# End of the last block in halves and three column groups, accumulators added earlier, norms by square root and reciprocal, gates by tanh

## The reference, cut to what matters

```python
mix = token_mixer(x, ...)          # ends in  sigmoid(ga) * (o @ w_branch_a) + sigmoid(gb) * (yc @ w_branch_b), then @ w_out
x = layer_norm(ALPHA * x + mix, ln1_g, ln1_b)                       # "first norm"
x = layer_norm(ALPHA * x + peer(x, ...), ln2_g, ln2_b)              # "second norm"
x = x + sigmoid(x @ ple_w_gate) * (p @ ple_w_proj)                  # "final gate"

def layer_norm(x, g, b):           # (x - mean) * rsqrt(var + 1e-5) * g + b
def peer(x, w_q, sub_keys, u, v):  # per token: 8 heads x 16 experts found by top-k search over product keys
    h = gelu(sum_d u[e, d] * x[d])             # for each of the 128 experts e of the token
    return sum_e softmax_weight[e] * h[e] * v[e, :]
```

## Time and profile before

| | |
|---|---|
| median of 3 runs | 1919.62 us (1918.05 to 1920.31) |
| the profiled execution, own time | 1921.58 us |
| its span | 1919.5 us |
| busy: PE, DVE, ACT, POOL | 1620.7, 1293.0, 814.6, 487.8 us |
| gathers (queue q0) | 536.90 MB of 655.38 MB moved |
| mean granted clock of PE | 0.956 of full speed |

### The profile page before, as it was taken

The page is one execution under the profiler, slowest core; times in us unless marked ns, Lnnn a source line. Parts: engine busy times, 40 slices in busy tenths (PEclk is TensorE's granted clock), DMA queues, the critical chain, the costliest instruction groups (busy, mean ns, idle before and its releaser), DMA issues.

```text
span 1919.5 us, 17005 instructions
## 1 busy us (share of the span) xinstructions
PE 1620.7 (84%) x5048; PEld 898.7 (47%) x5048; DVE 1293.0 (67%) x2758; ACT 814.6 (42%) x1954; POOL 487.8 (25%) x530
## 2 busy tenths in 40 slices
PE   8999989779999899688978767778787778878787
PEld 6888867675555557344434322233222223222223
DVE  4453575169987679777777777776666677666643
ACT  6566574132147312534434434443444444344432
POOL 0000000022222122232333333333333333333330
PEclk9999999889999999899989988999999999999998
DMA  5112256789999989899999999999999999999992
GB/s 204 52 63 87 88 219 263 274 353 416 393 386 401 370 306 379 359 419 384 414 371 418 404 414 411 382 416 372 422 413 422 421 373 420 384 422 422 421 421 97
DMA packets 93925, 655.38 MB, mean 341 GB/s; under 512 B 10256, under 2 KB 13840, under 8 KB 15632
## 3 DMA queue, kind: packets, MB, share of 16 engines
q0 software_dynamic: 73728, 536.90, 68.6%
q1 hardware_dynamic: 20112, 117.48, 15.8%
HBM read 652.24 MB, written 2.10 MB: 341 GB/s over the span
## 4 chain that ended last, share of the span: by engine, by line
PE 41%; DMA 31%; ACT 11%; DVE 11%; issue 4%; POOL 1%; SPq 0%; ACTq 0%; DVEq 0%; POOLq 0%
DMA uv<-in_pk_uv,idx 29%; PE psum L1624 11%; PE psum L1530 11%; PE psum L1386 4%; DVE uv L1257 4%; PE psum L1549 4%; PE psum L1592 2%; PE psum L1563 2%; PE psum L1501 2%; PE psum L1482 2%; DVE oT L1270 1%; ACT diag L807 1%; DMA raw<-in_w_branch_a 1%; ACT L795 1%; ACT coef L799 1%
## 5 line engine op out<-in xcount | busy, mean ns | idle before, releaser
L1624 PE MATMUL psum<-uv,diag 128*128 128x512 f32 x1424 | 732.1, 645 | 229.5 <-ACT diag L807 225.9
L1257 DVE CUSTOM_DVE_ANT_0 uv<-uv,psum 128x1024 f32<-128x1024 f32 x512 | 622.4, 1216 | 318.8 <-DMA uv<-in_pk_uv,idx 312.6
L573 POOL DMA_INDIRECT uv<-in_pk_uv,idx x512 | 484.3, 946 | 1387.8 <-DVE oT L1270 494.0
L1624 PEld LDWEIGHTS psum<-uv,diag 128*128 128x128 f32 x1424 | 263.1, 200 | 668.4 <-ACT diag L807 442.3
L795 ACT ACTIVATE gelu<-dots 128x1 f32<-128x1 f32 x512 | 103.5, 202 | 787.8 <-DVE dots L1257 785.9
L1530 PE MATMUL psum<-xT,raw 128*128 128x384 f32 x640 | 206.6, 486 | 0.0
L1270 DVE SCALAR_TENSOR_TENSOR oT<-uv,coef,oT 128x1024 f32<-128x1024 f32 x152 | 194.3, 1279 | 15.7 <-ACT coef L799 15.7
L1530 PEld LDWEIGHTS psum<-xT,raw 128*128 128x128 f32 x640 | 121.6, 190 | 84.5
L799 ACT ACTIVATE coef<-gelu,weight 128x1 f32<-128x1 f32 x512 | 150.9, 295 | 16.9 <-ACT gelu L795 0.2
L807 ACT ACTIVATE diag<-ident,coef 128x128 f32<-128x128 f32 x356 | 143.0, 402 | 11.7
L1386 PE MATMUL psum<-xTh,w_hi 128*128 128x512 f32 x256 | 105.4, 412 | 9.3 <-DVE xTl L984 9.3
(11 more groups left out here) (199 smaller groups left out, 1668.3 us busy)
## 6 DMA issues: line engine op xcount, KB each, us to landing
raw<-in_w_in SPq DMA_DIRECT2D x56, 1024.0 KB, 6.8
raw<-in_pk_w_q SPq DMA_DIRECT2D x16, 1024.0 KB, 8.8
raw<-in_w_branch_a SPq DMA_DIRECT2D x8, 1024.0 KB, 7.3
raw<-in_w_branch_b SPq DMA_DIRECT2D x8, 1024.0 KB, 6.8
raw<-in_w_out SPq DMA_DIRECT2D x8, 1024.0 KB, 10.1
uv<-in_pk_uv,idx POOLq DMA_INDIRECT x512, 9.8
w_gate<-in_ple_w_gate SPq DMA_DIRECT2D x1, 4096.0 KB, 13.8
x_raw<-in_x_t SPq DMA_DIRECT2D x4, 512.0 KB, 7.3
```

The source lines that it names most:

```text
L573: pool.indirect_dma_start(uv[:, r % UV, :], None, pk_uv, bass.IndirectOffsetOnAxis(idx[:, i % 2, j:j + 1], 0)).then_inc(row_in[r % UV], 16)
L1257: V.tensor_tensor_reduce(u, u, x_cur[:], 1.0, 0.0, ALU.mult, ALU.add, dots[:, r % 32:r % 32 + 1]).then_inc(dot_done, 1)
L1624: last = T.matmul(B[i][:], diag[:, n % DR, :], uv[:, r % UV, D + i * 512:D + (i + 1) * 512], start=(r in FIRST), stop=(k == BLOCK_ROWS - 1 ...
```

## The change

- **Gates.** The sigmoids of `unit_out` and of the final gate become tanh(x/2); since sigmoid(x) = (1 + tanh(x/2))/2, the multiplications by a gate become one instruction (gate + 1) times the other factor. The doubled `mix` of blocks 1 to 3 is met by `2.0 * ALPHA` and an epsilon of 4e-5 in their first norm (`twice`); the final gate's half is in the last addition. The sigmoids of the mixer ahead of the loop stay.
- **Norms.** `rstd_of` becomes `root_of` (one Sqrt on ACT) and a reciprocal on DVE, which stands in DVE's order just ahead of the shift.
- **Accumulators.** `add_acc` of blocks 1, 2 and 3 moves from row 126 of the block to rows 118, 44 and 44.
- **Halves.** PE signals `v_half` after the first 512 columns of a block's last row; `fin_sum` adds each half when it is there. In the last block the shift, the transposes and the start of the gate matmuls go by halves too.
- **Last gate in three groups** of 512, 256 and 256 columns: matmuls, tanh, multiplication, addition and store of one group after another, with the last group in bank 2.

```diff
-        ACC_ROW = [BLOCK_ROWS * (b + 1) - 2 for b in range(TB)]
+        ACC_ROW = [BLOCK_ROWS * b + t for b, t in enumerate((BLOCK_ROWS - 2, 118, 44, 44))]
+        LAST_PARTS = [(0, 512), (512, 768), (768, 1024)]
+        LAST_BANK = (6, 7, 2)
...
-            store(3)
-            sp.wait_ge(stored, 16 * TB)
+            for i, (d0, d1) in enumerate(LAST_PARTS):
+                sp.wait_ge(x3_done, TB + i)
+                sp.dma_start(ov[:, TB - 1, d0:d1], x2[:, d0:d1]).then_inc(stored, 16)
+            sp.wait_ge(stored, 16 * (TB + len(LAST_PARTS) - 1))
...
-                    nc.scalar.activation(t[:, c, P:], src, ACT.Sigmoid).then_inc(t_act, 1)
+                    nc.scalar.activation(t[:, c, P:], src, ACT.Tanh, scale=0.5).then_inc(t_act, 1)
...
-                nc.scalar.activation(rstd[:, 0:1], mean_var[:, 1:2], ACT.Ln, bias=eps_ln[:, 0:1]).then_inc(rst, 1)
-                act.wait_ge(rst, 2 * n + 1)
-                nc.scalar.activation(rstd[:, 1:2], rstd[:, 0:1], ACT.Exp, scale=-0.5).then_inc(rst, 1)
+                nc.scalar.activation(rstd[:, 0:1], mean_var[:, 1:2], ACT.Sqrt,
+                                     bias=eps_ln[:, twice:twice + 1]).then_inc(root, 1)
...
-                nc.scalar.activation(gate[:, i * 512:(i + 1) * 512], B[6 + i][:], ACT.Sigmoid).then_inc(g_sig, 1)
+                nc.scalar.activation(gate[:, i * 512:(i + 1) * 512], B[6 + i][:], ACT.Tanh, scale=0.5).then_inc(g_sig, 1)
...
-            for i in range(2):
-                gate_sigmoid(TB - 1, i)
+            for i, (d0, d1) in enumerate(LAST_PARTS):
+                act.wait_ge(g_mm, 2 * (TB - 1) + i + 1)
+                nc.scalar.activation(gate[:, d0:d1], B[LAST_BANK[i]][:, 0:d1 - d0], ACT.Tanh, scale=0.5).then_inc(g_sig, 1)
...
-                V.tensor_tensor(g, g, B[bank(r)][:, 0:n], ALU.mult).then_inc(t_dve, 1)
+                V.scalar_tensor_tensor(out=g, in0=g, scalar=1.0, in1=B[bank(r)][:, 0:n],
+                                       op0=ALU.add, op1=ALU.mult).then_inc(t_dve, 1)
...
+            def norm_rstd(n, root, rec):
+                dve.wait_ge(root, n + 1)
+                V.reciprocal(rstd[:, 1:2], rstd[:, 0:1]).then_inc(rec, 1)
...
-                dve.wait_ge(v_used, v_count(BLOCK_ROWS * (b + 1) - 1))
...
                 for i in range(2):
                     d = slice(i * 512, (i + 1) * 512)
+                    if i == 0:
+                        dve.wait_ge(v_half, b + 1)
+                    else:
+                        dve.wait_ge(v_used, v_count(BLOCK_ROWS * (b + 1) - 1))
                     V.scalar_tensor_tensor(out=x2[:, d], in0=x_of(b)[:, d], scalar=ALPHA, in1=B[i][:],
                                            op0=ALU.mult, op1=ALU.add).then_inc(acc_out, 1)
...
-                norm_shift(b, x2[:], ln2[1], x2_step, x2_rstd, x2_done)
+                norm_rstd(b, x2_root, x2_rec)
+                if b < TB - 1:
+                    norm_shift(b, x2[:], ln2[1], x2_step, x2_rec, x2_done)
+                else:
+                    for i in range(2):
+                        d = slice(i * 512, (i + 1) * 512)
+                        norm_shift(b, x2[:, d], ln2[1][:, d], x2_step, x2_rec, x2_done)
...
-                V.tensor_tensor(gate[:, d], gate[:, d], B[pb][:], ALU.mult).then_inc(fin_step, 1)
+                V.scalar_tensor_tensor(out=gate[:, d], in0=gate[:, d], scalar=1.0, in1=B[pb][:],
+                                       op0=ALU.add, op1=ALU.mult).then_inc(fin_step, 1)
...
-                V.tensor_tensor(x2[:], x2[:], gate[:], ALU.add).then_inc(x3_done, 1)
+                V.scalar_tensor_tensor(out=x2[:], in0=gate[:], scalar=0.5, in1=x2[:],
+                                       op0=ALU.mult, op1=ALU.add).then_inc(x3_done, 1)
...
-            for i in range(2):
-                fin_gate(TB - 1, i)
-            fin_add(TB - 1)
+            n = 2 * (TB - 1)
+            for i, (d0, d1) in enumerate(LAST_PARTS):
+                dve.wait_ge(g_sig, n + i + 1)
+                dve.wait_ge(p_mm, n + d0 // 512 + 1)
+                pb = B[P_BANK[1] + d0 // 512][:, d0 % 512:d0 % 512 + d1 - d0]
+                V.scalar_tensor_tensor(out=gate[:, d0:d1], in0=gate[:, d0:d1], scalar=1.0, in1=pb,
+                                       op0=ALU.add, op1=ALU.mult).then_inc(fin_step, 1)
+                dve.wait_ge(fin_step, n + i + 1)
+                V.scalar_tensor_tensor(out=x2[:, d0:d1], in0=gate[:, d0:d1], scalar=0.5, in1=x2[:, d0:d1],
+                                       op0=ALU.mult, op1=ALU.add).then_inc(x3_done, 1)
...
+                    if k == BLOCK_ROWS - 1 and i == 0:
+                        last.then_inc(v_half, 1)
...
             def x2_turn(b):
-                pe.wait_ge(x2_done, b + 1)
                 for kh in range(2):
+                    pe.wait_ge(x2_done, b + 1 + (kh if b == TB - 1 else 0))
...
-            for n in range(2 * KT):
-                gate_mm(TB - 1, n)
+            for i, (d0, d1) in enumerate(LAST_PARTS):
+                for k in range(KT):
+                    if i == 0 and k % 4 == 0:
+                        pe.wait_ge(x2T_done, 2 * (TB - 1) + k // 4 + 1)
+                    last = T.matmul(B[LAST_BANK[i]][:, 0:d1 - d0], x2T[:, k, :], w_gate[:, k, d0:d1],
+                                    start=(k == 0), stop=(k == KT - 1), skip_group_check=True)
+                last.then_inc(g_mm, 1)
```

More of the change, by code:

```diff
@@ L190, in build @@
         eps_rms = small("eps_rms", [1])
-        eps_ln = small("eps_ln", [1])
+        eps_ln = small("eps_ln", [2])
         psum = ctx.enter_context(nc.psum_tensor("psum", [P, 8, 512], F32))
@@ L227, in build @@
         ln1_in = sem("ln1_in")
[L228 removed]
+        ln_step, ln_var, ln_root, ln_rec = sem("ln_step"), sem("ln_var"), sem("ln_root"), sem("ln_rec")
+        x1_done = sem("x1_done")
         x1_cur = sem("x1_cur")
@@ L551, in _ @@
             pool.memset(eps_rms[:], RMS_EPS).then_inc(consts, 1)
-            pool.memset(eps_ln[:], LN_EPS).then_inc(consts, 1)
-            pool.wait_ge(consts, 9)
+            pool.memset(eps_ln[:, 0:1], LN_EPS).then_inc(consts, 1)
+            pool.memset(eps_ln[:, 1:2], 4 * LN_EPS).then_inc(consts, 1)
+            pool.wait_ge(consts, 10)
             pool.affine_select(out=ident[:], in_=ident[:], compare_op=ALU.not_equal, fill=1.0, base=0,
@@ L783, in x_current, with root_of @@
                     nc.scalar.activation(B[2 + i][:], x_of(b)[:, i * 512:(i + 1) * 512], ACT.Copy).then_inc(x1_cur, 1)
-            def rstd_of(n, var, rst):
+            def root_of(n, var, root, twice=False):
                 act.wait_ge(var, n + 1)
-                nc.scalar.activation(rstd[:, 0:1], mean_var[:, 1:2], ACT.Ln, bias=eps_ln[:, 0:1]).then_inc(rst, 1)
-                act.wait_ge(rst, 2 * n + 1)
-                nc.scalar.activation(rstd[:, 1:2], rstd[:, 0:1], ACT.Exp, scale=-0.5).then_inc(rst, 1)
+                nc.scalar.activation(rstd[:, 0:1], mean_var[:, 1:2], ACT.Sqrt,
+                                     bias=eps_ln[:, twice:twice + 1]).then_inc(root, 1)
             def row(r):
@@ L1130, in residual, with norm_stats @@
                 xs = x_of(b)[:, c * CW:(c + 1) * CW]
-                V.scalar_tensor_tensor(out=xs, in0=xs, scalar=ALPHA, in1=B[bank(r)][:, 0:CW],
+                V.scalar_tensor_tensor(out=xs, in0=xs, scalar=2.0 * ALPHA, in1=B[bank(r)][:, 0:CW],
                                        op0=ALU.mult, op1=ALU.add).then_inc(t_dve, 1)
-            def norm_stats(src, step):
+            def norm_stats(src, step, ready=None):
                 for i in range(2):
+                    if ready:
+                        dve.wait_ge(ready[0], ready[1] + i)
                     V.bn_stats(stats[:, i, :], src[:, i * 512:(i + 1) * 512]).then_inc(step, 1)
@@ L1144, in norm_scale, with norm_shift @@
                                        op0=ALU.subtract, op1=ALU.mult).then_inc(step, 1)
-            def norm_shift(n, dst, bias, step, rst, done):
+            def norm_rstd(n, root, rec):
+                dve.wait_ge(root, n + 1)
+                V.reciprocal(rstd[:, 1:2], rstd[:, 0:1]).then_inc(rec, 1)
+            def norm_shift(n, src_dst, bias, step, rec, done):
                 dve.wait_ge(step, 3 * n + 3)
-                dve.wait_ge(rst, 2 * n + 2)
-                V.scalar_tensor_tensor(out=dst, in0=dst, scalar=rstd[:, 1:2], in1=bias,
+                dve.wait_ge(rec, n + 1)
+                V.scalar_tensor_tensor(out=src_dst, in0=src_dst, scalar=rstd[:, 1:2], in1=bias,
                                        op0=ALU.mult, op1=ALU.add).then_inc(done, 1)
@@ L1164, in norm1_shift @@
             def norm1_shift(b):
-                norm_shift(b, tiled(x_of(b)), ln1[1], ln_step, ln_rstd, x1_done)
+                norm_rstd(b, ln_root, ln_rec)
+                norm_shift(b, tiled(x_of(b)), ln1[1], ln_step, ln_rec, x1_done)
             LOWEST = float(np.finfo(np.float32).min)
```

28 lines of the change are left out of this document (14 added, 14 removed).

## The result

The changed kernel takes 1899.49 us in the median of 6 runs (1892.8 to 1903.97), against 1919.71 for the kernel before (6 runs beside it, 1916.64 to 1920.31). The ratio is 0.9899, with a 95% interval from 0.9882 to 0.9915: 19.4 us faster by the ratio, 16 to 23 by the interval. The prediction was 1900.0, from 1890 to 1910. The profiled execution took 1898.09 us (span 1896.1), 23.5 less than the profiled one of before.

A forecast was written before the change was run, and what follows sets the result against it. No single bound: PE ahead of the row loop and during the mixer's matmuls, DMA in blocks two to four. Terms 0.45 + 3.7 + 4.5 + 1.4 + 1.5 + 3.0 + 5.1 = 19.7 us gave 1899.9 us for the median; range 1890 to 1910.

The forecast's parts named there:

- Bound and place: No single bound; in blocks two to four the loop can give time back only where DMA engines are not full.
- Root and reciprocal: All norms: net 1.5 us less per norm where ACT and DVE are late; 0.45 ahead of loop, 4.5 at block ends.
- the first norms: First norms of blocks 1 to 3: ACT taken as the bound, 3.7 us won of 3.8 idle DMA.
- `add_acc` and halves in the loop: Ends of blocks two and three: DVE's 0.77 us wait for PE ahead of `fin_sum` goes; 1.4 us in all.
- Clock at the ends of blocks two and three: PE's shorter pause may keep the clock up; bounds 0 and 3.0 us, middle taken, 1.5.
- Tanh: Behind two of the gates: tanh shares Gelu's table, both loads go; 3.0 us won of 4.8 idle DMA.
- The zero for the mixer's gates: Sixteen mixer gates lose two loads each, but PE is busy without a gap there; counted as zero.
- The last block: Tail: 1.6 before aggregation, 1.8 to the gate's first matmul, -0.1 gate matmuls, 1.3 to the store, 0.5 store; 5.1 us.
- the smaller store: Last store, 128 KB instead of 512 KB: 0 to 0.9 us less from issue to end, 0.5 taken.
- tanh needs a load of its own: Rival at the gates: tanh does not share Gelu's table, so that term gives no gain; chance 0.12.
- the tail gives back: Rival, last block: PE meets the lower clock for eight more gate instructions, 3.4 us lost, 1903.3; chance 0.10.
- The loop gives nothing: Rival: another late part, DVE, keeps the slots; only 0.45 and the tail are left, 1914.1; chance 0.09.

The follow-up runs named there:

- Kernel 10: Changed kernel with the three square roots of the first norms behind one table load at row 100; ratio 0.9883 to the kernel before.
- kernel 7: Changed kernel with `add_acc` of blocks 1 and 2 back at row 126 and the sum whole in blocks 0 to 2; ratio 0.9899 to the kernel before.
- kernel 1: Kernel before with square root and reciprocal in all eight norms, nothing else; ratio 0.9978 to the kernel before.
- 6: Changed kernel with all its tanh gates back to sigmoid; ratio 0.9924 to the kernel before.
- 5: Changed kernel with Ln and Exp back in all norms; ratio 0.9922 to the kernel before.
- 8: Kernel before with tanh in the final gates alone, the mixer's gates keeping sigmoid; ratio 0.9979 to the kernel before.
- kernel 2: Kernel before with tanh for sigmoid in the mixer's gates of blocks 1 to 3 and the final gates; ratio 0.9951 to the kernel before.
- 3: Kernel before with the last block alone changed, keeping Ln, Exp and sigmoid; ratio 0.9966 to the kernel before.
- 4: Kernel before with `add_acc` of blocks 1 and 2 at rows 118 and 44 and halves in blocks 0 to 2; ratio 0.9962 to the kernel before.
- 12: Kernel before with tanh in the mixer's gates of blocks 1 to 3 alone; ratio 0.9984 to the kernel before.
- kernel 9: Changed kernel with the block-end root at row 7 instead of 2, shift, transposes and gate five rows later; 1892.57 us, ratio 0.9865 to the kernel before.

## Why the prediction was right, and where it was not

The total, 19.7 against 19.4, lies this near by luck in part. It is a sum of terms of which some were too large and others too small by 2 us and more, and the profiled executions differ by 23.5.

- *Bound and place: right.* The loop gave time back only where the DMA engines were idle, at block ends and gates, and these were the places whose DMA shares rose.
- *Root and reciprocal: the price right, the first norms wrong.* Ahead of the loop, aggregation to shift took 2.17 us before and 1.72 after, the 0.45 of the term. At the second block's end PE's pause fell by 1.51, and by the groups the norms gave about 4 at the ends of blocks two and three, where 3.0 were predicted; at the first block's end, predicted 1.5, none is seen. The step that failed is "ACT is busy 18.57 of 20 us, so it is the bound" at the first norms: 3.7 predicted, 1.0 measured, 0.2 to 1.0 in the five kernels with this part. ACT's busy time there fell from 18.57 to 14.26 us, and the DMA share stayed at 0.81. DVE stood at 18.98 in the same row and then at 19.71, and both long waits of the gathers there end on DVE; so it is the likely bound, but no run took work from DVE at this place. Kernel 10 took four more loads from ACT there and moved 1.5 us, not to stay.
- *`add_acc` and halves in the loop: 1.4 predicted, about 2 by the groups at the ends of blocks two and three.* The medians don't decide: 7.3 alone, 0.0 beside the other parts (kernel 7), give or take 5. The wait of 0.77 went as said.
- *Clock at the ends of blocks two and three: 1.5 predicted, open.* PE's pause became 3.52 us, as worked out, and in the profiled execution the clock fell behind it both times. But in the five profiled executions with this pause (the whole, 1, 6, 7, 10) three of the ten were followed by four instructions in 1.98 us, the full clock, and seven by the lower one at first; the pauses of 5.03 were followed by the lower clock each time. The stretches with the full clock gained 1.6, 3.2 and 3.0 us and those with the lower one 1.4 to 4.7, so no gain can be put to it. At the first block's end the clock stayed up, which the term didn't count.
- *Tanh: shares the table, as taken; 3.0 was too small.* 4.8 beside the other parts, give or take 5. The failing step is that only two gates were counted. Behind the third, rows 408 to 432, the change gained 3.3, kernels 5, 7 and 8 with tanh there 2.7, 3.9 and 1.0 (kernel 2 lost 0.9), and those with sigmoid 0.0 to 0.3 (3, 4, 6) or 1.1 to 1.3 (12, 1). By the groups the second gate gave 2.0 and the third 1.6. The zero for the mixer's gates is neither shown nor refuted. The trace of before had idle DMA behind the third gate too, at the place that the earlier trace rows shows behind the other two:

```profile
1632.00:1652.00 20.00, 16.49 (x33) 6.57 (x32) 14.69 (x34) 6.57 (x21) 5.93 (x7) 0.90 0.90 331
```

- *The last block: 5.1 predicted, 6.7 measured.* 1.6, 1.8 and 1.3 came out as 1.7, 1.9 and 1.3. The gate's products gained 1.0 where -0.1 was taken, within the bounds given, since in this execution the lower clock met fewer of them; the smaller store gave 0.9, the upper bound of its term, for 0.5.

By stretches of the profile: block ends 8.3 us for 7.4 (4.5 + 1.4 + 1.5), tail 6.7 for 5.1, first norms 1.0 for 3.7, gates 4.9 (rows 280-312 and 408-432) for 3.0, and 2.5 at row 0 for 0.45. About 2 of these 2.5 are no part of the change: in the chain of waits 32 matmul instructions of `branch0` take 8.67 us before and 7.14 after, with nothing changed there.

Of the rivals, "tanh needs a load of its own" and "the tail gives back" are out by the trace. "The loop gives nothing" named DVE as the holder of the slots. At the first norms that may be so. At the block ends it isn't what happened: the loop gave time there, and PE's pause, which ends on ACT, shrank. The times of the first four rivals are the median's, not the profiled execution's as their heading says: "tanh needs a load of its own", for one, is 1901.9 + 3.0 = 1904.9 there. The signs came out as forecast where they could be read: the tail from the last diagonal to the end is 27.7 us, Gelu's line has 18 loads fewer and the lines of the gates 19, the granted clock is 0.961. Only the gather's wait fell to 6.37 us and not to 5.

## What to carry to other kernels

Here a ring of six buffers swallowed one stall of about 3 us for nothing and passed two in one place on, so price a stall by what stands beside it: kernel 9 has a load more at each block end than the changed kernel and is the faster one. Where two engines are both nearly full in a window, relieving one may show little (1.0 of 3.7 us here); look at both columns before naming the bound. Test each part alone and each left out, and keep in mind what all the test kernels share and how wide a difference of two intervals is: here 8 us of "overlap" between the parts may be either. Stretches of one profile are as uncertain; the same stretch over all test kernels, grouped by part, separated 4 us from 2.

## What the runs showed of the hardware

Tanh needs no table load between two Gelus, nor does it cost more than sigmoid (0.58 to 0.60 us for 512 columns). A table load costs its 1.28 us and no more than 0.02 beside it (1226.92 to Gelu at 1228.21). What the clock does behind a pause isn't settled by the pause's length. In the changed kernel PE's pauses of 3.52 us were followed by instructions at 0.81 to 0.83 us instead of 0.43 at both block ends, in kernel 1 the same pause by the full clock (1.98 us for four). In kernel 9 a pause of 1.91 was followed by the full clock (1.98 for four), one of 1.90 by 2.85 for four (at 1247.26) and one of 2.94 by 2.89. Behind 5.03 the clock was the lower one in every profiled execution. The last store's 128 KB in pieces of 1 KB took 2.2 us from issue to the end, 512 KB in pieces of 4 KB 3.1.
